# Meta keys ahead of the token keys, and the head sums of three tiles taken earlier, in a hybrid decoder step

## The reference

```
h = rms_norm(x) @ w_in             -> mq mk mv mo gates dq dk dv
mLSTM:      chunked matrix memory over mq, mk, mv with decays from the gates
attention:  a1 = softmax(q1 k1^T), a2 = softmax(q2 k2^T)   (causal, two maps per head)
            out = (a1 - lam * a2) @ dv                      (4 heads, 64 dims per map)
x = x + [rms_norm(hm) * sigmoid(mo), rms_norm(ha)] @ w_out
MoE:        group by argmax, two experts of eight in it, SwiGLU, weighted sum
y = rms_norm(x);  also returned: keys, values, matrix memory C, n, m
```

## Time and profile before

| | us |
|---|---|
| median of 3 runs | 657.62 |
| lowest and highest of them | 655.08, 664.13 |
| the profiled execution | 654.61 |
| its span, first to last instruction | 652.9 |

### The profile page before, as it was taken

The page is one execution under the profiler, slowest core; times in us unless marked ns, Lnnn a source line. Parts: engine busy times, 40 slices in busy tenths (PEclk is TensorE's granted clock), DMA queues, the critical chain, the costliest instruction groups (busy, mean ns, idle before and its releaser), DMA issues.

```text
span 652.9 us, 9092 instructions
## 1 busy us (share of the span) xinstructions
PE 594.0 (91%) x3397; PEld 324.3 (50%) x3397; DVE 252.2 (39%) x603; ACT 147.7 (23%) x430; POOL 122.0 (19%) x205
## 2 busy tenths in 40 slices
PE   4999899799899999999979976999999996999792
PEld 2544444345455565555535654655555553555341
DVE  2320048534333442357568478332112211121067
ACT  3110142333333355440022120101101100011012
POOL 2341006320022011110043111021421120210013
PEclk9999999999999999999989956999999997999797
DMA  8736155851512030018089878999999999999973
GB/s 290 220 98 197 46 182 172 282 169 50 212 38 92 3 130 0 9 64 247 22 330 397 284 295 316 419 415 416 400 419 419 422 420 421 422 418 421 414 313 139
DMA packets 55111, 163.60 MB, mean 251 GB/s; under 512 B 15253, under 2 KB 23574, under 8 KB 42394
## 3 DMA queue, kind: packets, MB, share of 16 engines
q1 hardware_dynamic: 45290, 145.77, 58.0%
q0 software_dynamic: 7552, 17.19, 8.0%
q10 hardware_dynamic: 2224, 0.04, 0.2%
HBM read 148.71 MB, written 23.24 MB: 263 GB/s over the span
## 4 chain that ended last, share of the span: by engine, by line
PE 64%; DMA 15%; DVE 8%; issue 7%; ACT 3%; POOL 2%; POOLq 0%; DVEq 0%; SPq 0%; ACTq 0%
PE bank L2106 13%; PE scores L2387 8%; PE bank L2103 8%; PE bank_t L2370 7%; PE bank_p L2370 6%; PE bank L2318 6%; DMA XHT<-in_w_down_e 5%; DMA WS<-in_w_down_e 5%; DMA MO<-in_cache_k,pages 2%; PE bank_p L2231 2%; DMA WS<-in_w_in 2%; PE bank L2360 2%; PE scores L2199 1%; PE bank_t L2341 1%; PE bank_t L2122 1%
## 5 line engine op out<-in xcount | busy, mean ns | idle before, releaser
L2106 PE MATMUL bank<-WS,XHT 128*128 128x512 f32 x192 | 88.8, 609 | 1.9 <-DMA WS<-in_w_in 1.4
L2103 PE MATMUL bank<-XHT,WS 128*128 128x512 f32 x192 | 85.0, 597 | 0.8 <-PE bank_t L2122 0.8
L2103 PEld LDWEIGHTS bank<-XHT,WS 128*128 128x128 f32 x192 | 35.7, 190 | 42.9 <-issue 42.6
L2106 PEld LDWEIGHTS bank<-WS,XHT 128*128 128x128 f32 x192 | 35.5, 193 | 42.3 <-issue 40.2
L2370 PE MATMUL bank_p<-WS,XHT 128*64 128x256 f32 x256 | 43.3, 381 | 1.6 <-DMA XHT<-in_w_up_e 1.2
L1021 POOL DMA_INDIRECT out_rows<-MVA,slot_ids x15 | 15.1, 1008 | 153.1 <-DVE MVA L1900 150.5
L2370 PE MATMUL bank_t<-WS,XHT 128*64 128x256 f32 x224 | 39.4, 381 | 0.2 <-DVE XHT L1883 0.2
L909 POOL TENSOR_SCALAR rr<-ss 128x1 f32<-128x1 f32 (+3 forms) x25 | 8.7, 348 | 140.3 <-ACT XHT L1302 41.1
L2370 PEld LDWEIGHTS bank_p<-WS,XHT 128*64 128x64 f32 x256 | 26.7, 137 | 14.0 <-DMA XHT<-in_w_up_e 1.7
L2387 PE MATMUL scores<-WS,FT 128*64 128x512 f32 x72 | 27.9, 671 | 5.6 <-DMA WS<-in_w_down_e 5.6
L2318 PE MATMUL bank<-WS,XHT 128*128 128x512 f32 x64 | 30.5, 624 | 1.0 <-DVE XHT L1702 1.0
(11 more groups left out here) (467 smaller groups left out, 996.5 us busy)
## 6 DMA issues: line engine op xcount, KB each, us to landing
WS<-in_w_gate_e SPq DMA_DIRECT2D x16, 1024.0 KB, 10.0
WS<-in_w_up_e SPq DMA_DIRECT2D x14, 1024.0 KB
WS<-in_w_down_e SPq DMA_DIRECT2D x14, 1024.0 KB
WS<-in_w_in SPq DMA_DIRECT2D x6, 2048.0 KB, 10.7
XHT<-in_w_up_e SPq DMA_DIRECT2D x10, 1024.0 KB
XHT<-in_w_down_e SPq DMA_DIRECT2D x9, 1024.0 KB
XHT<-in_w_gate_e SPq DMA_DIRECT2D x8, 1024.0 KB, 30.0
FT<-in_w_up_e SPq DMA_DIRECT2D x6, 1024.0 KB
```

The lines of the kernel that those rows point to most:

```text
L2103: mm = pe.matmul(PS[r][:, :], w[:, k, 128 * m:128 * (m + 1)], hT[:, k, 0:512], start=(k == 0), stop=(k == KC - 1))
L2106: mm = pe.matmul(PS[r][:, :], hT[:, k, 128 * m:128 * (m + 1)], w[:, k, :], start=(k == 0), stop=(k == KC - 1))
```

## The change

Two things are changed. First, dkT keeps the 16 meta keys in columns 0 to 15 and the token keys from column 16 on; its decode columns are not written any more. All that reads dk in transposed form (the transposes for the key output, the scores, the mask's place, the transposes of the mixture) follows, and the scores of a half-head come from one matmul for tiles 0 to 2 and two for tile 3 (512 and 16 columns). Second, in `ORDER`, `hs` of tiles 0, 1 and 2 moves ahead of `wa 3, 0` and waits for `mpa 3` alone; `on 0` and `on 1` move ahead of `wsk`, which now stands ahead of the evictions of `wa 3, 1` and `wa 4, 0` along with them.

```diff
-    order += more() + [("mpa", 3)] + more() + [("mpb", 3), ("wsk",)] + more()
-    order += [("hs", 0), ("hs", 1), ("on", 0), ("hs", 2), ("on", 1)] + more() + [("mdec2",), ("ot", 0)]
+    order += more() + [("mpa", 3), ("hs", 0), ("hs", 1), ("hs", 2)] + more() + [("mpb", 3), ("on", 0), ("on", 1), ("wsk",)]
+    order += more() + more() + [("mdec2",), ("ot", 0)]
...
+        def first_token(b):
+
+            return NMETA if b == "dk" else 0
@@ ScalarE, item acc @@
-                        ins = copy(feat[b][:, m, 0:512], src[:, :], scale)
+                        o = first_token(b)
+                        ins = copy(feat[b][:, m, o:o + 512], src[:, :], scale)
@@ ScalarE, item ft @@
-                    copy(feat[b][:, :, 512:ROWS], src).then_inc(freed["p"], 1)
+                    if b == "dk":
+                        copy(dkT[:, :, 0:NMETA], src[:, :, 0:NMETA]).then_inc(freed["p"], 1)
+                    else:
+                        copy(feat[b][:, :, 512:ROWS], src).then_inc(freed["p"], 1)
@@ ScalarE, items hsa and hs @@
+                    elif j < 3:
+                        drained(act, ("mpa", H - 1), "t")
                     else:
-                        drained(act, ("mpa", H - 1), "t")
                         drained(act, ("mpb", H - 1), "p")
@@ VectorE, item qk @@
-                    d0 = 128 * j if j < NT else 0
+                    d0 = NMETA + 128 * j if j < NT else 0
@@ TensorE, item tok @@
+                    o = first_token(b) + col(j)
...
-                        mm = pe.transpose(PS[r][:, 128 * (m - m0):128 * (m - m0 + 1)], feat[b][:, m, col(j):col(j) + 128],
+                        mm = pe.transpose(PS[r][:, 128 * (m - m0):128 * (m - m0 + 1)], feat[b][:, m, o:o + 128],
@@ TensorE, item qk @@
-                    for m in range(2):
-                        before(pe, item, ("Sa", "Sb")[m])
-                        r = slice(64 * m, 64 * m + 64)
-                        at_ = 0
-                        if j < NT:
-                            at_ = 128 * (j + 1)
-                            pe.matmul(Sps[0:n, m, 0:at_], dqT[r, h, c0:c0 + n], dkT[r, h, 0:at_], start=True, stop=True)
-                        if at_ == 512 and m:
-                            drained(pe, ("tp",) + UNITS[UIDX[j, h] - 1], "m")
-                        mm = pe.matmul(Sps[0:n, m, at_:at_ + NMETA], dqT[r, h, c0:c0 + n], dkT[r, h, 512:512 + NMETA],
-                                       start=True, stop=True)
-                        mm.then_inc(filled[("Sa", "Sb")[m]], 1)
+                    w = NMETA + (128 * (j + 1) if j < NT else 0)
+                    for b in ("Sa", "Sb"):
+                        before(pe, item, b)
+                    for a in range(0, w, 512):
+                        last = min(w, a + 512)
+                        for m in range(2):
+                            if a and m:
+                                drained(pe, ("tp",) + UNITS[UIDX[j, h] - 1], "m")
+                            r = slice(64 * m, 64 * m + 64)
+                            mm = pe.matmul(Sps[0:n, m, a:last], dqT[r, h, c0:c0 + n], dkT[r, h, a:last], start=True, stop=True)
+                            if last == w:
+                                mm.then_inc(filled[("Sa", "Sb")[m]], 1)
@@ TensorE, item tp @@
-                    at_ = 128 * (j + 1) if j < NT else 0
-                    pe.transpose(PS["m"][0:NMETA, 0:n], P[0:n, 0, at_:at_ + NMETA], ident[0:n, 0:n]).then_inc(filled["m"], 1)
+                    pe.transpose(PS["m"][0:NMETA, 0:n], P[0:n, 0, 0:NMETA], ident[0:n, 0:n]).then_inc(filled["m"], 1)
...
-                            mm = pe.transpose(PS["t"][:, 128 * i:128 * (i + 1)], P[0:n, 0, 128 * i:128 * (i + 1)], ident[0:n, 0:n])
+                            mm = pe.transpose(PS["t"][:, 128 * i:128 * (i + 1)], P[0:n, 0, NMETA + 128 * i:NMETA + 128 * (i + 1)], ident[0:n, 0:n])
```

## The result

The changed kernel takes 649.54 us, the median of 20 runs (644.12 to 655.22). The kernel before, run 20 times beside it, takes 653.86 us. The ratio is 0.9918 (95% interval 0.9896 to 0.9940): faster, by 0.8%, which is less than the 2% that the prediction counted as a change. The ratios and means in this document leave out executions more than 1.5% above the fastest of the same kernel (three of these twenty), so 0.9918 is not the quotient of the two medians, 0.9934. The kernel moved by 4.3 us by the medians and by 5.4 by the ratio, where 3.4 was forecast. The three runs of before that set the forecast's base have a median of 657.62 us, 3.8 above the median of the twenty.

What follows compares the result with a forecast made beforehand. TensorE's own queue bounds attention and the stretch after; the expert stage is a race between weights and matmuls. Keys 2.5 plus hand-over 0.9, clock 0, save 3.4 us: 657.62 becomes 654.2, range 649.8 to 659.8.

Steps and rivals of the forecast that it cites:

- The sum's base: Whole kernel: savings are taken from 657.62 us, the median of the runs shown; the profiled execution took 654.61.
- The keys, 2.5 us: Score steps, tiles 0 to 2: dropping narrow matmuls saves 0.20 to 0.21 us in each of twelve; bounds 1.3 to 3.2.
- rival D: Score steps: narrow records were cheap, 0.11 us a step; gain 2.2 us, 655.4; chance 0.62 together with the forecast.
- softmax chain: Attention: mask, maximum, exponentials and mixing move forward with the score steps, their projection cover kept; no separate gain or cost.
- Tile 3, zero: Tile 3's score steps keep two pieces and the same wait; zero gain, 0.1 us either way for four steps.
- The hand-over, 0.9 us: Attention to output projection: earlier sums of squares and gating start the first output product 0.9 us earlier; bounds 0 to 2.1.
- Rival C: Hand-over: late sums hold VectorE in on(1), evictions end 3.1 us later; kernel slower, 658.2 us; chance 0.07.
- The clock, price 0: First output products: the low clock stays, so no gain; worth 1.9 us if it goes; bounds minus 1.9 to plus 1.7.
- rival A: First output products: the clock stays up; gain 5.3 us, median 652.3; chance 0.18.
- The expert stage passes the gain on: Expert stage: an earlier TensorE frees buffers and starts the weight stream earlier, so it does not just wait longer.
- rival B: Expert stage: the weight stream starts no earlier and swallows the gain; gain 0 to 1 us, 657; chance 0.13.
- The sum: Whole kernel: 2.5 us of keys plus 0.9 of hand-over, 3.4 us or 0.5%; median 657.62 becomes 654.2.

Runs made afterwards that it cites:

- run 20: Not a label but part of "run 20 times": the kernel before, unchanged, run 20 times beside the changed kernel; median 653.86 us.
- keys alone: Changed kernel with the old work order and gate, so only the meta keys first and fewer score matmuls; 651.16 us (ratio 0.9976), then 652.13 us (0.9948).
- narrow twice: Kernel before, with each narrow score matmul of tiles 0 to 2 issued twice in a row on its own row half; 668.28 us, ratio 1.0188.
- both halves side by side: Kernel before, with each step's score matmuls ordered wide, wide, narrow, narrow across the two row halves; 654.03 us, ratio 0.9993.
- then twice: Kernel before, with score matmuls ordered wide, wide, narrow, narrow and the narrow pair of tiles 0 to 2 issued twice; 659.71 us, ratio 1.0082.
- before, TensorE filled: Kernel before, plus twelve identity products of 128 columns in TensorE's hand-over waits, into a bank nobody reads again; 653.69 us, ratio 0.9957.
- order alone: Kernel before with only the change's two order lines and gate, keys as before; 653.30 us (ratio 0.9991), then 651.50 us (0.9945).
- evictions first: Changed kernel with key scaling moved behind the evictions of the last two attention products; 647.67 us, ratio 0.9921.
- and turn 1 later: Changed kernel, key scaling behind the last two evictions and head sum 1's turn behind the first output product; 648.97 us (ratio 0.9884), then 649.00 us (0.9922).
- four old traces named above: Traces with the old key order: two of the kernel before (654.61 us profiled; 654.91 us median), the first of order alone (653.30), and before, TensorE filled (653.69).

## Why the prediction was right or wrong

The landmarks of the traces, in us, start to start. Hand-over: small tile's attention product to first output product. Output: from there to the small tile's output product. Expert stage: from its first matmul (L2370 in the kernel before) to the last matmul of the program.

| kernel | hand-over | output | expert stage |
|---|---|---|---|
| before; again | 6.90; 6.89 | 39.62; 40.78 | 246.5; 248.3 |
| keys alone, twice | 6.91; 6.90 | 39.62; 39.61 | 245.2; 245.3 |
| narrow twice; both halves side by side; then twice | 6.90; 6.90; 6.89 | 40.10; 40.89; 40.40 | 245.1; 245.2; 244.8 |
| before, TensorE filled | 6.90 | 37.93 | 245.5 |
| order alone, twice | 5.73; 5.73 | 37.93; 37.93 | 247.4; 245.2 |
| change, three times | 5.73; 5.73; 5.73 | 39.34; 37.93; 37.92 | 247.0; 245.1; 245.2 |
| evictions first | 3.85 | 37.91 | 246.3 |
| and turn 1 later, twice | 3.84; 3.84 | 38.36; 38.36 | 246.6; 247.0 |

**The sum's base: failed, and the largest part of the miss.** The step took the saving from 657.62, the median of three runs, though it had the profiled execution at 654.61 beside it. Twenty runs have a median of 653.86. The same steps on that base give 650.5, inside the range and 0.9 from the time.

**The keys, 2.5 us: right in kind, about twice too large in the steps.** Measured per step 0.11 to 0.12 in eleven of the twelve and nothing in one, together 1.2 us. That is about the lower bound that the prediction set, and rival D. The doubled pair says how the reading failed. A narrow pair does take 0.22 to 0.23 us in its place, so the number taken was a true one. But when it goes, the wide pair stands last, directly ahead of a projection that uses all 128 rows, and there it is dearer. Wide pairs of 128, 256 and 384 columns took 0.32, 0.54 and 0.75 us ahead of a narrow one. Those of 144, 272 and 400 columns ahead of a projection take 0.44, 0.66 and 0.87. The sixteen columns are 0.03 of that, by the prediction's estimate; 0.09 to 0.10 belong to being last. The prediction took out the group and did not ask what its neighbour would then pay.

What the 0.09 us are made of stays open. The Trainium skill has a rule for such places, in "TensorE: Matmul & The Clock Gate", Part 3, The mechanism: a weight load overlaps running matmuls only where it goes to other rows of the array. The projection's first load touches both halves, the narrow ones only one. But the trace does not agree with the rule as it stands: at 158.62 both loads of a product on all 128 rows are over after 0.30 us, beside the product's own first record on the same rows, and eight such records take 3.44 us, 0.43 each. The price by the LDWEIGHTS section of the same page of the Trainium skill, which the prediction set beside its own, was 0.43 us a step; the trace shows 0.11, and four loads of a step within 0.30 us beside its matmuls.

The prediction also put the softmax chain at nothing, since its cover was kept. It was not fully covered: in tile 2 TensorE waited 0.3 to 1.0 us for a mixture in the four old traces named above, and 0.4 at most in the nine with the new keys. That is the further 0.5 us of the keys, so they brought about 1.7 us in all.

**Tile 3, zero: right.** 217.80 to 219.38 us in the changed trace, 1.58 us, and 1.58 before (219.79 to 221.37).

**The hand-over, 0.9 us: right, measured 1.2.** 6.90 to 5.73 us, and in every trace with the new order. Each link stands as written: sums behind the first half's evacuation, no wait for a root, key scaling between the gating and the evictions, the eviction of the small tile last. The 0.3 more is VectorE's: the two gatings took 2.66 us (322.76 to 325.42) where 2.84 were summed, the evictions 2.29 where 2.5 were. Rival C is refuted: VectorE left on(1) at 325.5, and its wait was gone in every trace.

**The clock, price 0: failed; rival A was the case.** All seven traces with the old order and no fill, those with doubled narrow matmuls among them, have the low clock over the first output products. Of the nine with the new order eight have the full one; the ninth is the trace taken first. (Four of the eight are versions with a shorter wait or with products in it; of the five with the change's own hand-over four have the full clock.) In the seven the output stretch is 1.7 to 3.0 us longer than 37.93, 2.2 in the mean; in the five it is longer in one, by 1.4, or 0.3 in the mean. So the clock brought about 1.9 us. The runs agree: 50.0 us at the low level (0.4) before, 45.8 (0.7) in the change, 45.8 (0.8) with the order alone, 48.1 (1.0) with the keys alone. That is 4.2 us less, worth at most 2.1 us of time. The prediction's argument against it, that the quiet stretch shrinks by only 0.9 of 5 us, was sound about the wait and wrong about the outcome: a quarter less was enough. The filled kernel shows the cause directly: the same wait with work in it, and the full clock behind it. The Trainium skill's rule in "TensorE: Matmul & The Clock Gate", Part 1, that activity releases the low level, leaned to this side, and the traces agree. A single execution can still go either way: TensorE did the same work ahead of the first output product in all five traces with the change's own hand-over, and one of them had the low clock behind it.

**The expert stage passes the gain on: right, rival B refuted.** The last column changes by a microsecond or two without regard to how early the stage began. The last matmul of the change starts 2.9 to 9.4 us earlier than that of before's first trace, the beginning of the expert stage 3.5 to 8.0.

**The sum.** Rival A's 5.3 us come near the 5.75 in part by luck: its keys term of 2.5 is 0.8 too large, and its hand-over term of 0.9 is 0.3 too small. By the measured terms, 1.2 of score steps, 0.5 of TensorE's wait in tile 2, 1.2 of hand-over and 1.9 of clock are 4.8 of the 5.75 us (0.44) measured. The 0.9 us left are about two errors and stay unplaced. For the keys alone the 1.7 us and up to 0.9 of clock meet the 2.6 (0.55) measured.

**No better version.** Evictions first and the later turn shorten the path to the expert stage by 1.3 to 1.9 us, and their times (648.1 with an error of 0.8, 649.0 with 0.4) can't be told from the change's. Where it is given back was not settled. Nor was a version tried that gives the first output product another bank.

## What to carry to other kernels

Price a removed group by the start of what follows it, with and without it, and ask what its neighbour pays when it becomes the last of its kind. Where TensorE waits some microseconds ahead of a dense stretch, read the granted clock behind the wait first: shortening the wait by a quarter brought about 1.9 us of clock on average, where the shorter wait itself was 1.2 us, and filling the old wait with products into a bank that nobody reads brought as much. Before a forecast in tenths of a per cent, take the base from the profiled execution or many runs; three runs can be half a per cent off.

## What the runs showed of the hardware

- Four narrow fp32 records (two matmuls of 16 columns, one on each row half) and their weight loads take 0.22 us behind a wide pair. Doubled one behind the other on each half, they also kept the wide matmuls of the two halves from running side by side, and a step grew by 0.54, 0.75 and 0.97 us at 128, 256 and 384 columns.
- A score pair directly ahead of a 128-row product takes 0.09 to 0.10 us longer than ahead of another 64-row pair, at 144, 272 and 400 columns alike (estimate: 0.03 us for the sixteen columns taken off).
- 3.3 us of dummy products in a 5 us wait kept TensorE at 2.4 GHz behind it, in the one trace taken; without them and with that wait it fell to 1.2 GHz in seven of seven traces.
- The low clock also comes by chance. Ten of the seventeen traces, with either order of the keys, have a stretch of it between tile 0's first score step and the small tile's attention product. In the changed kernel's first trace it stood over a projection of tile 1:

```profile
166.00:169.00 3.00, 3.00 (x4) 1.39 (x5) 1.62 (x5) 1.05 (x4) 0.00 (x0) 0.50 0.91 369
```

From the first score step of tile 1 to that of tile 2 this trace needs 28.3 us, and the change's second trace and both of the keys alone 26.6. One such fall costs 1.7 us, more than all twelve shorter steps bring.
